# One gate build for the dense token pair, with half of the gates kept off chip, and a token-tile order for the output product

## What is computed

```python
x = x + gate1 * _rmsnorm(mix, n_mix_post)            # mix = merged @ w_out
h = _rmsnorm(x, n_ffn_pre) * (1 + scale2) + shift2
x = x + gate2 * _rmsnorm(_peer(h, ...), n_ffn_post)

q = (xb @ w_query).reshape(t, PEER_HEADS, 2, HALF_KEY)
s = jnp.einsum('thik,hink->thin', q, sub_keys)       # two halves of 128 keys
v_half, i_half = lax.top_k(s, TOPK)                  # 16 of each
cand = v_half[..., 0, :, None] + v_half[..., 1, None, :]
top_v, top_pos = lax.top_k(cand, TOPK)               # 16 experts per head
g = jax.nn.softmax(top_v, axis=-1)
act = jax.nn.gelu(jnp.einsum('thkd,td->thk', expert_u[idx], xb))
out = jnp.einsum('thk,thkd->td', g * act, expert_v[idx])
```

## Time and profile before

| | us |
|---|---|
| median of 3 runs | 2974.27 (2971.63 to 2975.97) |
| the profiled execution, its time | 2972.99 |
| its span, first to last instruction | 2971.0 |
| TensorE busy | 2500.6 (84%) |
| VectorE busy | 1930.8 (65%) |
| GpSimd busy | 1041.6 (35%) |
| ScalarE busy | 605.5 (20%) |
| mean granted TensorE clock | 0.888 |

### The profile page before, as it was taken

One profiled execution on the slowest core, in us unless ns is written; L12 is line 12 of the kernel. 1 busy time (PEld: TensorE's weight loads), 2 busy tenths in 40 slices (PEclk: granted clock), 3 DMA queues, 4 the chain that ended last, 5 costly groups with the idle time before them and its releaser, 6 DMA issues.

```text
span 2971.0 us, 27796 instructions
## 1 busy us (share of the span) xinstructions
PE 2500.6 (84%) x9370; PEld 1619.2 (55%) x9370; DVE 1930.8 (65%) x3598; ACT 605.5 (20%) x1568; POOL 1041.6 (35%) x864
## 2 busy tenths in 40 slices
PE   6988888899899966994799998555999999555997
PEld 1444554454456433763388887544666666454443
DVE  0337776641114576678779976999677751999765
ACT  0124254331111111110212112332000002332000
...
GB/s 272 186 50 36 29 49 35 43 44 157 205 170 206 163 253 228 270 399 334 284 186 163 243 251 327 228 237 261 394 401 397 405 357 142 232 232 261 400 404 285
DMA packets 233513, 684.87 MB, mean 231 GB/s; under 512 B 20528, under 2 KB 45232, under 8 KB 233136
## 3 DMA queue, kind: packets, MB, share of 16 engines
q0 software_dynamic: 110592, 402.70, 37.4%
...
## 4 chain that ended last, share of the span: by engine, by line
PE 27%; DVE 15%; DMA 6%; issue 3%; POOL 1%; ACT 1%; ACTq 0%; DVEq 0%; POOLq 0%
PE bank L1023 14%; PE bank L1053 7%; DVE arena L1871 5%; DMA arena<-in_peer_v,arena 5%; PE bank L987 4%; DVE arena L1849 3%; DVE arena L2039 2%; DVE arena L2032 1%; PE bank L828 1%; POOL arena L1498 1%; POOL arena L1506 1%; PE bank L999 0%; DMA arena<-in_peer_u,arena 0%; DVE arena L1805 0%; DVE arena L1802 0%
## 5 line engine op out<-in xcount | busy, mean ns | idle before, releaser
L1498 POOL DMA_INDIRECT arena<-in_peer_u,arena x384 | 477.6, 1244 | 1051.6 <-DVE arena L1849 708.6
L828 PE MATMUL bank<-arena 128*128 128x512 f32 (+1 forms) x1600 | 565.1, 515 | 20.1 <-DMA arena<-in_w_in 7.2
L1871 DVE SCALAR_TENSOR_TENSOR arena<-arena 128x1024 f32<-128x1024 f32 x381 | 489.9, 1286 | 128.2 <-DMA arena<-in_peer_v,arena 119.7
L1506 POOL DMA_INDIRECT arena<-in_peer_v,arena x384 | 448.6, 1168 | 306.5 <-DVE arena L1871 216.3
L1849 DVE CUSTOM_DVE_ANT_0 arena<-arena 128x1024 f32<-128x1024 f32 x384 | 467.7, 1221 | 118.8 <-DMA arena<-in_peer_u,arena 116.0
L1053 PE MATMUL bank<-arena 128*128 128x512 f32 x1024 | 454.1, 596 | 16.9 <-DVE arena L2050 16.9
L828 PEld LDWEIGHTS bank<-arena 128*128 128x128 f32 x1600 | 307.5, 193 | 272.9 <-issue 229.0
L1023 PE MATMUL bank<-arena 128*128 128x256 f32 x2048 | 452.9, 379 | 0.7 <-ACT arena L1359 0.7
L1023 PEld LDWEIGHTS bank<-arena 128*128 128x128 f32 x2048 | 389.0, 190 | 81.0 <-issue 30.6
L1042 PE MATMUL bank<-arena 128*128 128x64 f32 x1024 | 232.5, 421 | 196.1 <-ACT arena L1416 196.1
L1042 PEld LDWEIGHTS bank<-arena 128*128 128x128 f32 x1024 | 220.8, 327 | 208.2 <-ACT arena L1416 198.2
(11 more groups left out here) (235 smaller groups left out, 2374.0 us busy)
## 6 DMA issues: line engine op xcount, KB each, us to landing
arena<-in_peer_ut SPq DMA_DIRECT2D x128, 512.0 KB
arena<-in_peer_v SPq DMA_DIRECT2D x128, 512.0 KB
arena<-in_w_in SPq DMA_DIRECT2D x22, 2048.0 KB
arena<-in_w_ada SPq DMA_DIRECT2D x12, 2048.0 KB
arena<-in_w_ssd_out SPq DMA_DIRECT2D x8, 2048.0 KB
arena<-in_w_query SPq DMA_DIRECT2D x8, 2048.0 KB
arena<-in_w_fourier SPq DMA_DIRECT2D x4, 2048.0 KB
arena<-in_w_out SPq DMA_DIRECT2D x4, 2048.0 KB
```

The lines of the kernel that those rows point to most:

```text
L828: last = mm(bank[q % 5][:, 0:cols], rows_of(k), w[:, k, :], start=(k == 0), stop=(k == k_tiles - 1))
L1498: nc.gpsimd.indirect_dma_start(urow[U_SLOT[k]], None, a["peer_u"], bass.IndirectOffsetOnAxis(ap=entries(IDX, k), axis=0)).then_inc(u_in[U_ ...
L1506: nc.gpsimd.indirect_dma_start(vrow[V_SLOT[k]], None, a["peer_v"], bass.IndirectOffsetOnAxis(ap=entries(IDX, k), axis=0)).then_inc(v_in[V_ ...
L1871: STT(pv, vrow[slot], w, pv, ALU.mult, ALU.add).then_inc(s("vc_used"), 1)
```

## The change

1. The output product goes tile by tile, in the order 3, 4, 1, 2, both halves of a tile one after the other. VectorE adds positions first and then does per tile: two steps, `add_mix`, two steps, `make_h2`. Transposes lie between the products, and the first query units of tiles 3 and 4 ahead of the last tile's transposes. Q0 and Q1 are loaded when all output products are done.
2. There is one build, ahead of stage 3. Comparisons of i are 128 wide, the weight is multiplied in by GpSimd (one instruction per unit), TensorE makes 128 columns per token, in three pairs of banks. The lower 64 are multiplied into `Aw` as before, now in two instructions of 256. The upper 64 are copied by ScalarE into a staging tile and written off chip, in 8 transfers of 1 MB. They come back in 16 transfers of 0.5 MB (pieces of 512 bytes), and GpSimd multiplies them into the new blocks of `Aw` one by one, 20 blocks behind nominal progress (`MULT_LAG`).
3. The build holds 12 steps, then 104 nominal ones to the end of stage 3, the rest behind it. `top` no longer copies its scores.
4. The staging tile takes four of the six block slots. SP waits for the last write before it loads the first V block.

```diff
-APART_BUILD = [1 + u % 2 for u in range(UNITS)]
-APART_BETWEEN = 86
+APART_BUILD = [int(u % 8 in (1, 4, 7)) for u in range(UNITS)]
+APART_BETWEEN = 104
...
+GROUPS, IN_GROUP = 8, 2 * P // 8
+CHUNK = 4
+MULT_LAG = 20
...
+        at.setdefault(START_BETWEEN + (MULT_LAG + n) * APART_BETWEEN // HALF, []).append(n)
...
 @@ SP
-            for n in range(len(BLOCKS)):
+            def load_gates(c):
+                if c >= 2:
+                    sp.wait_ge(s("gm_done"), CHUNK * (c - 1))
+                sp.dma_start(gates_in[c % 2], far[:, :, CHUNK * c:CHUNK * c + CHUNK, :]).then_inc(gates_sem[c % 2], 16)
+            for n in range(HALF):
                 load_block(n)
+            for q in range(GROUPS):
+                sp.wait_ge(s("gs_staged"), 4 * q + 4)
+                sp.dma_start(gates_far[q], staged[q % 2].rearrange("p i t -> p (i t)")).then_inc(staged_out[q % 2], 16)
+            for q in range(2):
+                sp.wait_ge(staged_out[q], 8 * GROUPS)
+            for n in range(HALF, len(BLOCKS)):
+                load_block(n)
+                passed = (n - HALF) // 2 if n < 3 * HALF else HALF + (n - 3 * HALF) // 2
...
+                if n % 2 and passed >= MULT_LAG + 7 and (passed - MULT_LAG - 7) % CHUNK == 0:
+                    c = next(chunks, None)
+                    if c is not None:
+                        load_gates(c)
 @@ TensorE
-            for j in range(2):
-                job("l", f"WO{j}", m_lhs)
...
+            for n in range(4):
+                out_of_tile(WO_ORDER[n])
+                if n >= 2:
+                    turn_h2(n - 2)
+            turn_h2(2)
...
+            queries(0, 0)
+            queries(1, 0)
+            turn_h2(3)
+            queries(0, 1)
+            queries(1, 1)
...
                 for t in range(UNIT):
-                    last = mm(bank[6 + u % 2][:, HALF * t:HALF * t + HALF], hot_j[u % 2][:, t, :], hot_i[u % 2][:, t, :],
-                              start=True, stop=True)
+                    last = mm(bank[PAIRS[u % 3][t // 4]][:, P * (t % 4):P * (t % 4) + P], hot_j[u % 2][:, t, :],
+                              hot_i[u % 2][:, t, :], start=True, stop=True)
 @@ v_block
+                if i >= HALF:
+                    pe.wait_ge(s("gm_done"), i - HALF + 1)
 @@ ScalarE
-            def weigh_i(g, u):
-                act.wait_ge(s("ieq_done"), UNITS * g + u + 1)
-                for t in range(UNIT):
-                    one = hot_i[u % 2][:, t, :]
-                    last = A(one, one, ACT.Copy, scale=turned_w[:, 2, UNIT * u + t:UNIT * u + t + 1])
-                last.then_inc(s("ihot_done"), 1)
+            def take_gates(u):
+                if u >= 8 and u % 4 == 0:
+                    act.wait_ge(staged_out[u // 4 % 2], 16 * (u // 8))
+                for q in range(2):
+                    act.wait_ge(s("g_done"), 2 * u + q + 1)
+                    t0 = (UNIT * u + 4 * q) % IN_GROUP
+                    last = A(staged[u // 4 % 2][:, :, t0:t0 + 4],
+                             bank[PAIRS[u % 3][q]][:, :].rearrange("p (t i) -> p i t", t=4)[:, HALF:, :], ACT.Copy)
+                last.then_inc(s("gs_staged"), 1)
 @@ GpSimd
-            rows_of_apart(START_1)
-            build(0)
-            rows_of_apart(APART_BETWEEN)
-            build(1)
-            rows_of_apart(ASTEPS)
+            rows_of_apart(START_1)
+            pool.wait_ge(s("tw_out"), 1)
+            def weigh_i(u):
+                pool.wait_ge(s("ieq_done"), u + 1)
+                TT(hot_i[u % 2], hot_i[u % 2],
+                   turned_w[:, 2, UNIT * u:UNIT * u + UNIT].unsqueeze(2).broadcast_to([P, UNIT, P]),
+                   ALU.mult).then_inc(s("ihot_done"), 1)
+            def gate_block(n):
+                pool.wait_ge(s("s_out"), HALF + n + 1)
+                pool.wait_ge(gates_sem[n // CHUNK % 2], 16 * (n // CHUNK // 2 + 1))
+                part = Aw[:, n, :].rearrange("p (g t) -> p g t", g=GROUPS)
+                TT(part, part, gates_in[n // CHUNK % 2][:, :, n % CHUNK, :], ALU.mult).then_inc(s("gm_done"), 1)
+            weigh_i(0)
+            weigh_i(1)
+            for u in range(UNITS):
+                rows_of_apart(APART_BUILD[u])
+                if u + 2 < UNITS:
+                    weigh_i(u + 2)
+            for j in range(START_BETWEEN, ASTEPS):
+                rows_of_apart(1)
+                for n in MULTS_AT.get(j, []):
+                    gate_block(n)
 @@ VectorE
-            for i in range(4):
-                beside("l", "WO0", i)
...
-            for t in LAT4:
+            for n, t in enumerate(WO_ORDER):
+                beside("l", "WO0", n)
                 add_mix(t)
-                beside("l", "WO1", t - 1)
+                beside("l", "WO1", n)
                 make_h2(t, mix(t), h2a[:, t - 1, :] if t in APART else mix(t))
...
+                for q in range(2):
+                    part = Aw[:, :, UNIT * u + 4 * q:UNIT * u + 4 * q + 4]
+                    TT(part, part, bank[PAIRS[u % 3][q]][:, :].rearrange("p (t i) -> p i t", t=4)[:, 0:HALF, :],
+                       ALU.mult).then_inc(s("g_done"), 1)
+            def build():
+                equal(0)
+                equal(1)
+                for u in range(UNITS):
+                    apart_steps(APART_BUILD[u])
+                    gate_unit(u)
+                    if u + 2 < UNITS:
+                        equal(u + 2)
...
-            build(0)
-            apart_steps(APART_BETWEEN)
-            build(1)
+            build()
             apart_steps(ASTEPS)
```

234 lines of the change are left out of this document (128 added, 106 removed).

## The result

The changed kernel takes 3035.5 us (median of 4 runs, 3033.3 to 3039.1), the kernel before 2973.4 in the runs beside it: 1.0215 times as long, 95% interval 1.0203 to 1.0228. The forecast was "slower, 2993 us". The direction was right; the loss is 62 us and not 20, and it lies inside the range given. Profiled execution after: span 3032.7 us.

The account below looks back on a forecast made before the run. VectorE bounded the old builds, TensorE and DMA the rest. Forecast: build to 2078, S blocks to 2545, V blocks to 2765, then 139 + 8 + 60 to 2972, tail 17.6: span 2990, time 2993; own range 2970 to 3020, overall 2937 to 3052.

Parts of the forecast that it names:

- Output product tile by tile: Lead-in before the build: queries end 12 us earlier, and the build starts at 1838.5 where it came at 1849.65.
- Cycle of the build: Single build: 4.5 us per unit of 8 tokens, 7.6 us per step of row gathers, last gate at 2078.
- The exclusion between VectorE and GpSimd: Build: GpSimd's multiply does not run beside VectorE's second comparison; without this 3.95 us per unit in place of 4.5.
- TensorE's unit grows with its columns: Rival, build: TensorE's unit takes 7.3 us, cycle 6.3, adding 56 us, so 3049; chance 0.10.
- Staging: After the build: off-chip writes cost nothing but for the last MB; TensorE starts at 2090, 12 us later.
- Between, the price of a load of gates: Stretch after the build: each load of gates takes 1.75 us and costs rows 2.8 us, 13 of them counted.
- gathers held by gate loads: Rival, stretch after the build: GpSimd's rows queue behind gates waiting for loads, +50 to 70 us, 3050; chance 0.08.
- the end of the S blocks: End of the stretch after the build: step 156 reached at 2545, 455 us where TensorE alone needs 443.
- The end with both rows: After the last V blocks: 49 steps bounded by GpSimd's issue at 2.83 us, 139, plus 8 for two top-k.
- The end with v rows only: Last stretch: 40 v rows over four slots, 6 us per round, 1.5 each, 60 us; adds end at 2972.
- The byte count that I used as a cross-check: All after the build: 448 rows, 192 blocks and the gates take 871 us after 2078, giving 2949.
- TensorE stays last, 2783: Rival, kernel's end: one build falls off the path, ending at 2765 + 17.6 = 2783; given no chance.

## Why the prediction was right or wrong, point by point

**Output product tile by tile: right.** The first comparison comes at 1836.5, forecast 1838.5. Alone, the part gives 14 us, by ratio.

**Cycle of the build: right, for a partly wrong reason.** 4.65 us per unit in the kernel as changed, forecast 4.5; 7.2 per step, forecast 7.6; last gate at 2070.4, forecast 2078, the sum being 8 us high. The reason given for a step, that the row stands behind the multiply and cannot be issued before VectorE waits, is shown by the rows three steps ahead: 63 us of the build. The exclusion between VectorE and GpSimd is also there, in both directions: a dot of 1.22 reads 2.91 beside a multiply, and a multiply of 1.9 reads 2.81 where the second comparison is still to come. The Trainium skill's rule (SBUF — State Buffer, section "SBUF: two separate sides") agrees with that row. But I priced TensorE at 3.7 us in every unit. Twelve of the 32 took 3.4 to 3.8, each after an idle time of over 8 us such as the 8.90 at 1882.53; of the other 20 two took 3.6 and 3.7 and the rest 2.05 to 3.1; the mean is 2.9 (92.02 / 32). With 2.9 in its place the sum gives 8.2, or 4.1 per unit: that 4.5 came so near to the 4.65 is luck in part. The rival "TensorE's unit grows with its columns" (7.3) is thereby out.

**Staging: right.** TensorE starts at 2086.0, forecast 2090.

**Between, the price of a load of gates: too high, by how much stays open.** 1.4 us, forecast 2.8, is measured for loads that go in 4096 byte packets. For the changed kernel's own, packet times give the estimate of 1.83; 13 of them make 24 and not 36.

**Between, "gathers held by gate loads": the step that failed first.** I put the rival at 0.08 because "the buffers are double and a load has 28 us". The load has 28 us of TensorE's time, but it is issued when TensorE has passed a block, and wanted when the steps have reached it. I had not set the two paces side by side for the third piece: wanted at 2252, issued at 2276.55. The waits cost 25 us (both ways of shortening them give that), not the rival's 50 to 70; the short ones seem to be slack. That step 207 comes at 2773.8, forecast 2765, only 9 us late, is luck: 25 for the waits, less 4 for the earlier start, would make 21, and the other 12 are what the loads were overpriced, if the estimate of 24 for them holds. The hit on the end of the S blocks, 2544.7 for 2545, is luck as well, since 152 steps had begun there and not 156.

**The end with both rows: too cheap.** 162 us, forecast 147. I took GpSimd's issue as the bound, 2.83 per step, and 8 us for two selections. Outside the selections a step took some 3.0, and over two of them the dots stand 12 us apart instead of 3: with 16 x 2.45 + 9.4 = 48.6 us of work in the 53 of a group, VectorE has no room to catch up. Moving both selections ahead of TensorE's end shortened this stretch by 22 us, so they had cost 22 and not 8: 14 of these 15 us.

**The end with v rows only: too cheap.** 79 us, forecast 60. A round of four places takes 8 and not 6. Three of the 19 us are my rounding: 1.24 + 3.9 + 1.2 is 6.34, and there are ten rounds. With ten places the adds take 10 us less, and what remains goes at GpSimd's issue every 1.60. In the forecast the issue was 1.24, from a row without VectorE beside it. 19 us.

These are 9, 15 and 19: 43 of the 43 us between the forecast span (2990) and the one measured (3032.7). (They are differences between marks along one chain, so they must add up; the runs above are what ties each to a cause.) **The step of the prediction that failed** is thus the term for the end: 147 + 60 us forecast, 162 + 79 measured, 34 of the 43. Beside it stands the overlap of the gate loads, taken as hidden and worth 25 us, most of which other errors made good. The order of events stood: a full chain of waits in the build, rows last, TensorE done long before. What failed was the size of an end with VectorE, GpSimd and the DMA at 0.6 to 0.9, none of them saturated, which I had costed with each one's best number. The byte count that I used as a cross-check (2949) was the warning: it was 23 us off already, and the true gap to it is 66.

**"TensorE stays last, 2783": rightly given nothing.** TensorE ended at 2773.3, and the last weighted add 241 us later.

**What the change got for its price.** The two old builds took 218 and 220 us (the prediction has 225 for the first, which is wrong) and held 96 steps, 2.34 each; by subtraction they would be 213 without them, which no run shows. The new one, without steps, takes 136. That is a gain of some 77 us, and the product order 14 more. It was spent on twelve steps at 8.2 us (98 us, by the difference of the two builds) and on 84 steps that now run where they cost more. Given back to ScalarE, the same single build beats the two.
